# Samples' values in four column groups, compressed turns earlier, and the last projection chunk of layer 1 in another order

## What is computed

```python
z = rmsnorm(x) @ w_in                       # 2864 columns
q, kc, vc, ks, vs, kw, vw, gate, bgate = split(z)
gates = sigmoid(bgate)                      # 3 per head
o_cmp = softmax(q . compress(kc)) @ compress(vc)
o_sel = softmax(q . ks[selected blocks]) @ vs[selected blocks]
o_win = softmax(q . kw[window]) @ vw[window]
o = gates[0] * o_cmp + gates[1] * o_sel + gates[2] * o_win
y = x + (o * silu(gate)) @ w_out
```

## Time and profile before

| what | us |
|---|---|
| time, median of three runs | 977.55 (976.17 to 978.6) |
| profiled execution, time | 977.28 |
| profiled execution, span from first to last instruction | 975.6 |
| PE busy | 921.6 |
| DVE busy | 475.1 |
| ACT busy | 293.3 |
| POOL busy | 232.2 |

### The profile page before, as it was taken

How to read it: one execution, slowest core, us unless ns; L and a number is a source line. 1 busy time by engine, 2 the same in 40 slices (tenths; PEclk the granted TensorE clock), 3 DMA queues, 4 the chain that set the end, 5 groups by cost and what they waited for, 6 DMA issues and landing times.

```text
span 975.6 us, 15843 instructions
## 1 busy us (share of the span) xinstructions
PE 921.6 (94%) x5202; PEld 497.5 (51%) x5202; DVE 475.1 (49%) x965; ACT 293.3 (30%) x716; POOL 232.2 (24%) x321
## 2 busy tenths in 40 slices
PE   6999999999899999999999999998888888899998
PEld 3544444444455543454565766566444444556444
DVE  1157778779345552122234172715667776556211
ACT  5101111103454550032101111425555565445100
POOL 0000223210033330430424242001334443234000
PEclk9999999999999999999999999998999998999999
DMA  9142665593254567772414232020211231131211
GB/s 352 57 167 101 226 233 177 193 287 80 45 155 148 156 220 256 220 179 92 143 34 144 73 99 84 16 80 12 65 50 54 74 103 69 48 92 57 89 44 44
DMA packets 86070, 117.59 MB, mean 121 GB/s; under 512 B 21006, under 2 KB 49886, under 8 KB 85678
## 3 DMA queue, kind: packets, MB, share of 16 engines
q1 hardware_dynamic: 66432, 80.96, 25.7%
q0 software_dynamic: 9920, 27.31, 9.5%
q10 hardware_dynamic: 9648, 8.41, 2.7%
HBM read 108.68 MB, written 11.36 MB: 123 GB/s over the span
## 4 chain that ended last, share of the span: by engine, by line
PE 87%; DVE 5%; DMA 3%; ACT 3%; issue 1%; SPq 1%; ACTq 0%; DVEq 0%
PE ps L719 26%; PE ps L976 11%; PE ps L982 6%; PE ps L1269 6%; PE ps L999 4%; PE ps L728 3%; PE ps L1150 3%; PE ps L1161 3%; PE ps L1038 3%; PE ps L914 3%; PE ps L1226 2%; DMA arena<-cache_sb_v 2%; PE ps L892 2%; PE ps L864 1%; PE ps L1016 1%
## 5 line engine op out<-in xcount | busy, mean ns | idle before, releaser
L719 PE MATMUL ps<-wring,arena 128*128 128x512 f32 x448 | 198.4, 602 | 1.5 <-issue 1.5
L719 PEld LDWEIGHTS ps<-wring,arena 128*128 128x128 f32 x448 | 85.2, 192 | 105.8 <-issue 105.7
L667 POOL TENSOR_TENSOR z<-z,work 128x1024 f32<-128x1024 f32 (+1 forms) x64 | 80.2, 1253 | 200.5 <-DVE work L1983 199.7
L976 PE MATMUL ps<-wring,z 128*128 128x512 f32 (+2 forms) x320 | 108.4, 494 | 0.0
L1501 ACT ACTIVATE z<-ps,work 128x512 f32<-128x512 f32 (+3 forms) x128 | 66.6, 527 | 70.3 <-DVE work L1975 58.4
L1324 ACT ACTIVATE z<-ps 128x512 f32<-128x512 f32 (+1 forms) x64 | 27.4, 433 | 181.8 <-PE ps L719 147.5
L976 PEld LDWEIGHTS ps<-wring,z 128*128 128x128 f32 x320 | 55.4, 192 | 44.5 <-issue 42.9
L358 POOL DMA_DIRECT2D arena<-cache_sb_k x64 | 34.4, 537 | 167.4 <-DVE work L1618 143.1
L1823 DVE TENSOR_TENSOR arena<-ps,consts 128x512 f32<-128x512 f32 x32 | 30.4, 1024 | 83.9 <-PE ps L1016 83.9
L1512 ACT ACTIVATE arena<-ps 128x512 f32<-128x512 f32 (+3 forms) x128 | 48.9, 438 | 31.6 <-PE ps L1150 31.6
L1975 DVE TENSOR_REDUCE work<-ps 128x1 f32<-128x512 f32 (+3 forms) x128 | 56.9, 486 | 2.2
(11 more groups left out here) (317 smaller groups left out, 1271.0 us busy)
## 6 DMA issues: line engine op xcount, KB each, us to landing
wring<-w_in SPq DMA_DIRECT2D x12, 2048.0 KB, 9.7
arena<-cache_sb_k POOLq DMA_DIRECT2D x64, 256.0 KB, 3.0
arena<-cache_sb_v SPq DMA_DIRECT2D x64, 256.0 KB, 3.5
wring<-w_out SPq DMA_DIRECT2D x3, 2048.0 KB, 7.8
arena<-cache_sel_k SPq DMA_DIRECT2D x64, 64.0 KB, 1.8
consts<-cache_sel_v SPq DMA_DIRECT2D x64, 64.0 KB, 1.8
consts<-aux SPq DMA_DIRECT2D x1, 2299.5 KB, 16.3
xres<-x_prompt SPq DMA_DIRECT2D x4, 512.0 KB, 10.2
```

Source lines behind the costliest of these rows:

```text
L667: nc.gpsimd.tensor_tensor(P_u(n), P_u(n), bc(coef(n).unsqueeze(2), [P, 2, (NT - n % NT) * P]), ALU.mult).then_inc(n_scaled, 1)
L719: mm = pe.matmul(ps[:, t, 0:width], stat, mov, start=(k == 0), stop=(k == KT - 1))
L976: mm = pe.matmul(ps[:, bank, at:at + w], normed1(k, t), wring[:, slot, k, lo:lo + w], start=(k == 0), stop=(k == KT - 1))
```

## The change

Four things.

1. **Last projection chunk.** The two small tiles come first, then the rows of the samples, then the two tiles for the output gates. The sigmoid of the branch gates becomes an exp on ACT with an addition and a reciprocal on DVE. The first turn of the queries moves from step 22 to step 21, the first scores from 23 to 22, and both lose a wait or trade it for one of ACT. SP sends the samples' gates when DVE has finished them.
2. **Order within a unit.** On PE `cmp_scores` (j = 0) and `turn_cmp` (j = 4) come right behind `scores`; on ACT the copy of the turned compressed weights comes before `copy_p`; on DVE `cmp_max` and the first key copy come before the mix product and `cmp_weights`.
3. **Samples' softmax and values.** Mask, softmax, exps and the three turns come two units later. The values of sample 0 move from unit 45 to 47, of 6 from 58 to 59; all are now two units apart.
4. **Values in four column groups.** The matmul for page m of a group writes rows 32 m to 32 m + 31, so four follow each other in different quarters of the array; DVE keeps all 128 rows per sample pair (`o_acc`), and a new step, `sample_fold`, adds the four parts by four matmuls with a 0/1 matrix `fold` after the last unit.

The core of the diff:

```diff
-            VALUE_STEPS = {45: 0, 47: 1, 49: 2, 51: 3, 53: 4, 55: 5, 58: 6, 61: 7}
-            PTURN_STEPS = {41: 0, 42: 1, 43: 2}
+            VALUE_STEPS = {47: 0, 49: 1, 51: 2, 53: 3, 55: 4, 57: 5, 59: 6, 61: 7}
+            PTURN_STEPS = {43: 0, 44: 1, 45: 2}
...
-                sp.wait_ge(bank_free, 5 + 80)
+                sp.wait_ge(heads_ready, 3)
...
+                        turn_q(0)
...
                     if s == 22:
-                        turn_q(0)
-                    if s == 23:
-                        pe.wait_ge(bank_free, 5 + 5 * 15 + 2)
                         scores(0)
...
+                        if c == 5 and t == 2:
+                            project_rows(n, slot, xnT_ready, 5, W1 - c * CH, lhs=normed1_rows)
                         if c == 0:
                             pe.wait_ge(xnT_ready, 5 + t + 1)
                         pe.wait_ge(bank_free, n * 5 + (t + 1))
...
                         elif c == 3 and t < 2:
                             by_tokens(slot, t, 2 * t, 0, 2 * P, 0)
                             mm = by_tokens(slot, t, 2 * t + 1, 0, 2 * P, 2 * P)
-                        elif c == 5 and t >= 2:
-                            by_tokens(slot, t, 2 * t - 4, 2 * P, 3 * HN, 0)
-                            mm = by_tokens(slot, t, 2 * t - 3, 2 * P, 3 * HN, 3 * HN)
+                        elif c == 5 and t < 2:
+                            by_tokens(slot, t, 2 * t, 2 * P, 3 * HN, 0)
+                            mm = by_tokens(slot, t, 2 * t + 1, 2 * P, 3 * HN, 3 * HN)
                         else:
-                            mm = by_gates(slot, t, t * P)
+                            mm = by_gates(slot, t, (t - 2 if c == 5 else t) * P)
                         mm.then_inc(mm_done, 1)
                         between(4 * c + t)
-                    project_rows(n, slot, xnT_ready, 5, min(CH, W1 - c * CH), lhs=normed1_rows)
-
-                pe.wait_ge(bank_free, 5 + 5 * 15 + NT)
+                    if c < 5:
+                        project_rows(n, slot, xnT_ready, 5, CH, lhs=normed1_rows)
+
+                pe.wait_ge(bank_free, 5 + 80)
                 scores(1)
-                pe.wait_ge(bank_free, 5 + 80)
...
                         for m in range(4):
                             n = 4 * q + m
-                            mm = pe.matmul(ps[rows_b, 7, (q // 2) * P:(q // 2 + 1) * P], PT1[:, n * P + rows_b.start:n * P + rows_b.stop],
-                                           vsets[b % 2][q][:, m * P:(m + 1) * P], start=(n in (0, 8)), stop=(n in (7, 11)))
+                            mm = pe.matmul(ps[32 * m:32 * m + 32, 7, (q // 2) * P:(q // 2 + 1) * P],
+                                           PT1[:, n * P + rows_b.start:n * P + rows_b.stop],
+                                           vsets[b % 2][q][:, m * P:(m + 1) * P], start=(q != 1), stop=(q != 0))
                     mm.then_inc(sv_used, 1)
+
+                def sample_fold():
+
+                    take(7, *marks_dve.at("sv_sum"))
+                    for j in range(NB // 2):
+                        mm = pe.matmul(ps[32 * j:32 * j + 32, 7, 0:2 * P], cst("fold"), o_acc[:, j], start=True, stop=True)
+                    mm.then_inc(*marks_pe.next("sv_fold"))
 
                 for n in range(NUNIT):
                     i, j = n // 8, n % 8
                     if n + 2 < NUNIT:
                         scores(n + 2)
+                    if j == 0:
+                        cmp_scores(i)
+                    if j == 4:
+                        turn_cmp(i)
                     if i < 4:
                         for b, q in KEY_STEPS.get(j, [])[0:1]:
                             sample_keys(2 * i + b, q)
-                    if n == 35:
+                    if n == 37:
                         sample_mask()
                     if n in PTURN_STEPS:
                         sample_turn(PTURN_STEPS[n])
...
                         cmp_values(i)
                     if n >= 1:
                         turn_p(n - 1)
-                    if j == 0:
-                        cmp_scores(i)
                     if i < 4:
                         for b, q in KEY_STEPS.get(j, [])[1:2]:
                             sample_keys(2 * i + b, q)
                     if j == 2 and i + 1 < HN // 2:
                         turn_q(i + 1)
-                    if j == 4:
-                        turn_cmp(i)
                 turn_p(NUNIT - 1)
-                for n in range(NUNIT - 3, NUNIT):
+                values(NUNIT - 3)
+                sample_fold()
+                for n in range(NUNIT - 2, NUNIT):
                     values(n)
 
...
+                        if c == 5 and t == 2:
+                            evict_rows(c, [(2 * P, 2 * P + 3 * HN, ACT.Exp, -1.0), (0, 2 * P, ACT.Silu, 1.0)])
...
-                        elif c == 5 and t >= 2:
-                            ins_ = nc.scalar.activation(z[:, pair, BG:W1], ps[:, t, 0:2 * 3 * HN].rearrange("p (t c) -> p t c", t=2), ACT.Sigmoid)
+                        elif c == 5 and t < 2:
+                            ins_ = nc.scalar.activation(z[:, pair, BG:W1], ps[:, t, 0:2 * 3 * HN].rearrange("p (t c) -> p t c", t=2), ACT.Exp, scale=-1.0)
...
-                    if n >= 1:
-                        copy_p(n - 1)
                     if j == 4:
                         act.wait_ge(nc_turned, i + 1)
                         nc.scalar.activation(p_cmpT, ps[:, 7, :], ACT.Copy).then_inc(nc_T, 1)
+                    if n >= 1:
+                        copy_p(n - 1)
...
+                        dve.wait_ge(bank_free, 5 + 5 * 15 + 3)
+                        for g in (z[:, 0:NT, BG:W1], z[0:NB, NT, BG:W1]):
+                            st.done(TS(g, g, 1.0, None, ALU.add))
+                            rec = nc.vector.reciprocal(g, g)
+                            rec.then_inc(heads_ready, 1) if g.shape[0] == NB else st.done(rec)
...
-                        TS(o_s[rows_b], ps[rows_b, 7, 0:2 * P], mine, None, ALU.mult).then_inc(sv_T, 1)
+                        TS(acc, ps[:, 7, 0:2 * P], mine, None, ALU.mult).then_inc(sv_T, 1)
                     else:
-                        STT(o_s[rows_b], ps[rows_b, 7, 0:2 * P], mine, o_s[rows_b], ALU.mult, ALU.add).then_inc(sv_T, 1)
+                        dve.wait_ge(sv_T, b)
+                        STT(acc, ps[:, 7, 0:2 * P], mine, acc, ALU.mult, ALU.add).then_inc(sv_T, 1)
...
+                    if j == 0:
+                        cmp_max(i)
+                    if i < 4:
+                        for b, q in KEY_STEPS.get(j, [])[0:1]:
+                            sample_keys(2 * i + b, q)
                     if j == 2 and i:
                         mix(i - 1)
                     if j == 2:
                         cmp_weights(i)
-                    if i < 4:
-                        for b, q in KEY_STEPS.get(j, [])[0:1]:
-                            sample_keys(2 * i + b, q)
-                    if n in (36, 37, 38):
-                        sample_softmax(n - 36)
+                    if n in (38, 39, 40):
+                        sample_softmax(n - 38)
                     if n in PTURN_STEPS:
                         sample_turn(PTURN_STEPS[n])
                     if n in VALUE_STEPS:
                         sample_values(VALUE_STEPS[n])
-                    if j == 0:
-                        cmp_max(i)
...
-                dve.wait_ge(sv_T, NB)
+                dve.wait_ge(*marks_pe.at("sv_fold"))
```

More of the change, by code:

```diff
@@ L55 @@
        ("own_group", G), ("group_sum", NB * G), ("cmp_own", NB * NCB), ("spread", P),
-       ("forced", NSB), ("block_no", NSB), ("own_sample", 2), ("cmp_neg", NT * NPB), ("cmp_one", NT * NPB),
+       ("forced", NSB), ("block_no", NSB), ("own_sample", 2), ("fold", 2 * HN), ("cmp_neg", NT * NPB), ("cmp_one", NT * NPB),
        ("tri_neg", P), ("ones_neg", P), ("strict", P), ("strict_neg", P), ("ret_decay", H * P), ("q_decay", H), ("k_decay", H),
@@ L110, in constants @@
     put("own_sample", (i[:, None] % (2 * HN)) // HN == np.arange(2)[None, :])
+    put("fold", i[:, None] % (2 * HN) == np.arange(2 * HN)[None, :])
     put("cmp_own", np.where(i[:, None] // HN == np.arange(NB * NCB)[None, :] // NCB, 0, NEG))
@@ L274, in build @@
         p_impT = z[:, NT, P_OFF + 512:P_OFF + 768].rearrange("p (j c) -> p j c", j=2)
-        o_s = work[:, 528:784]
+        o_acc = z[:, NT, P_OFF:P_OFF + NPG * P].rearrange("p (j c) -> p j c", j=NB // 2)
         o3 = arena[:, 7232:7616]
@@ L1453, in fetch @@
                         nc.scalar.activation(cvT[:, HB:N_CMP], ps[:, 7, 0:HN1], ACT.Copy).then_inc(cvT_ready, 1)
-                    if s == 22:
-                        act.wait_ge(nq_turned, 1)
-                        nc.scalar.activation(qTs[:, 0], ps[:, 7, :], ACT.Copy, scale=SCALE).then_inc(nq_T, 1)
                     if s == 21:
```

34 lines of the change are left out of this document (18 added, 16 removed).

## The result

The changed kernel takes 970.86 us, median of seven runs (967.82 to 975.11); the kernel before, run beside it, 976.17 (973.91 to 980.36). The ratio is 0.994, 95% interval 0.992 to 0.996: 4 to 8 us less. The forecast was 968.5, with a range of 962 to 974. The sign and the range held, and so did the mechanism but for one term of the sum; the gain was 5.3 us instead of 8.8.

The account below looks back on a forecast made before the run. PE carries 87% of the chain; SP's 48 page loads are nearly the bound. Sample 7 at 891.8 plus tail 11.8 puts the output projection at 903.6 instead of 912.38: 977.28 - 8.8 = 968.5 us, range 962 to 974.

Parts of the forecast that it names:

- SP as the bound: Attention's second half: SP loads samples 2 to 7 at 1.10 us a page; PE waits some 14 us.
- The waits of pairs 0 to 3: Attention, head pairs 0 to 3: copies moved ahead cut PE's waits, -6.2 us, bounds -3 to -10.
- The seam: Layer 1's projection to attention: new wait 0.8, later wait 3.8 instead of 4.17; sum +0.5 us.
- The softmax: Samples' softmax two units later: old waits go, others come, 9.4 us in all; sample 0's values at 835.8.
- 1.5 for stretched matmuls: Samples' softmax stage: 1.5 us for matmuls stretched behind waits, part of the 9.4 us.
- rival D: Samples' values: waits keep PE's clock low; costs from 2.9 us of an interval's work, 996 us if all; chance 0.04.
- The tail: Sample 7 to output projection: 12.17 minus 2.0, plus 0.5 for the fold, plus 1.1 for lower clock: 11.8 us.
- A: Samples' value pages: SP is not the bound, pages in 0.75 us or less; time 953.4 us; chance 0.06.
- C: Samples' values: the four groups don't overlap, samples 0 and 7 keep 2.83 us; time 972.5 us; chance 0.06.
- B: Around the samples' softmax: waits come back one for one, sample 0 at 841; time 973.7 us; chance 0.12.

Follow-up runs that it names:

- third buffer: Changed kernel with the free key-page place as a third set for the samples' value pages, so 40 pages instead of 48 follow sample 0: 963.69 us.
- fixed pages: Changed kernel reading the value pages of samples 2 to 7 at fixed page numbers, without the page-table lookup (a probe, not usable): 954.06 us.
- one column group: Samples' values put back into one column group, without the fold: 974.95 us against the changed kernel, 966.50 us against the fastest kernel then (950.78).
- order back: Changed kernel with compressed scores, turns, maxima and copies, and the key copy, back in their old places in the unit: 975.61 us.
- exps earlier: Changed kernel with the samples' softmax steps and exps one unit earlier and SP gathering scores before the value pages of samples 0 and 1: 967.27 us.
- both: Changed kernel with the third buffer for value pages and the old units for the samples' softmax and values together: 956.34 us.
- gather first: Kernel with third buffer and old softmax units, plus scores gathered before value pages of samples 0 and 1 and samples' softmax and exps one unit earlier: 950.78 us.
- Steps back: Changed kernel with the samples' mask, softmax, exps, turns and values back in their old units: 965.56 us.

## Why the prediction was right, and where it was not

Distances between the same points of the chain, in us; the forecast, what the trace of after has, and the difference:

| step of the sum | forecast | measured | off by |
|---|---|---|---|
| seam, first tile to third scores | 42.57 + 0.5 | 43.40 | +0.3 |
| third scores to pair 4 | 114.26 - 6.2 | 108.35 | +0.3 |
| pair 4 to sample 0's values | 51.2 | 53.64 | +2.4 |
| sample 0 to sample 7 | 56.0 | 56.19 | +0.2 |
| sample 7 to output projection | 11.8 | 12.37 | +0.6 |

Together 3.8: from the first tile to the output projection the change saves 5.0 us (278.93 to 273.95) instead of 8.8, close to the 5.3 between the medians. The other 1.8 in this one pair of profiles lies ahead of the change.

- **SP as the bound: right.** The row is unbroken at 1.10 us a page, PE waits 12.7 us (14 forecast), and third buffer, fixed pages and the two runs with one column group show from four sides that it, and not the values, set the end.
- **The waits of pairs 0 to 3: right.** In unit 2 of a pair the wait for the key copy is 0.33 instead of 1.56, and the next one 0.72 instead of 1.21 (0.9 forecast); pair 0's query turn waits 1.49. 5.9 of 6.2 came.
- **The seam: right in kind.** 0.75 and 3.84 are the 0.8 and 3.8 of the sum. Its whole effect is too small for the times to confirm.
- **The softmax: this step failed, by its term for stretched matmuls.** The replay of the queues found the waits: 0.64, 1.32, 3.05 and 1.64 against 1.3, 1.3, 3.2 and 2.1. With another 0.5 us they sum to 7.2, less than the 7.9 of the forecast, and the remaining work is 41.6 against 41.8. But the "1.5 for stretched matmuls" measured 4.9. The prediction gave no row for it; in the same stage of before it had itself counted 3.1, and there the longest wait stood right ahead of sample 0's values, while here two long waits stand 6.6 us apart. In order back and exps earlier, where the waits of the stage are nearly the same or 1.2 us less, sample 0 came earlier by 3.4 to 3.9 us more than the waits explain, and the clock is what differs. This is the mechanism of rival D, in a place where I had not looked for it: ahead of SP's row, where it counts.
- **The tail.** The low clock behind the last page's wait (0.79 and 0.86 in the slices from 890 to 900) costs 1.4 instead of 1.1 (10.95 us in the three kernels that wait for no page at the end: fixed pages, both, gather first), and the fold 0.3 more than I put.
- **What the prediction did not weigh.** It took the two units by which the samples move back as part of the stage's work, and asked only whether waits come back. Two units are some 6.5 us of PE work put ahead of sample 0, at the head of the chain that the same text calls the bound. Steps back shows the price: 5.3 us. So the move ate most of what the compressed turns saved (5.9 us), and what was left, 0.6%, is not much more than the 4.1 us of the values.

Of the rivals, A and C are refuted (1.10 us a page; 0.86 us a sample), B is not borne out: waits came back around the softmax, but 7.2 us in all, less than the 7.9 of the sum; what made the stage 53.64 instead of 51.2 is the clock. D is refuted as a forecast, since the kernel is not slower, and right about the clock. Under SP's row it came near its condition once: behind the wait ahead of sample 5 the slice from 875 to 880 ran at 0.57, and only 0.66 us of waiting was left ahead of sample 6. The Trainium skill, "TensorE: Matmul & The Clock Gate", Part 1, says that activity releases a throttled default. The slices agree as far as they go: 0.50 behind the idle stretch, 1.00 again once PE is dense.

## What to carry to other kernels

Once a queue's row of transfers is the bound, write down what starts it: every step put ahead of that start costs in full, and a step that runs beside the row costs nothing while the row stays the bound. So shorten what leads to the start (here: softmax early, scores gathered first, a third buffer) before speeding up the matmuls beside it; the same edit of the values was worth 4 us in one kernel and 16 in the other. Price a wait of PE together with the clock behind it.

## What the runs showed of the hardware that I had not expected

- Of the 1.10 us that SP takes to issue a DMA whose page number comes from a table, 0.6 is the page number: 53.0 us for 48 of them, against 24.4 with fixed numbers, when the 9.5 us in which SP waits for buffers are taken from the row of 33.9. More than half of an issue-bound row goes without moving fewer bytes.
- Four column groups of 32 issue 24 matmul instructions of 128 columns in 0.86 us, 36 ns each, against 118 ns in one group.
- An equal sum of PE's waits (7.2 and 7.3 us) had 4.9 us of stretched matmuls behind it in one order and about 1.0 in another (49.91 less 7.3 of waits and 41.6 of work). Which feature of the order decides is not settled: the wait of 3.05 is the same in both, and the next one is 1.64 in one place against 0.75 and 0.36 in two.
- The scatter between runs of one kernel goes with the clock: in the seven runs of the changed kernel the mean granted clock of TensorE was 0.970 in the longest, 975.1 us, and 0.984 in the shortest, 967.8. A difference below some 3 us needs the trace's distances, not two single times.
